# A two-layer hybrid decoder step on Trainium2: the gathered tokens' gelu values fetched as rows of 128 floats and picked out on VectorE, with filled products and the modulation in two column groups

## What is computed

```python
mod = (jax.nn.silu(c) @ p["w_ada"][l] + p["b_ada"][l])[:, None, :]
sh1, sc1, gt1, sh2, sc2, gt2 = jnp.split(mod, 6, axis=-1)
...
sv, si = lax.top_k(s, PEER_TOPK)
cand = sv[:, :, 0, :, None] + sv[:, :, 1, None, :]
best, pos = lax.top_k(cand.reshape(...), PEER_TOPK)
g = jax.nn.softmax(best, axis=-1)
act = jax.nn.gelu(jnp.einsum("thkd,td->thk", u_tab[eidx], xb).astype(jnp.float32))
return jnp.einsum("thk,thkd->td", (g * act).astype(xb.dtype), v_tab[eidx])
```

## Time and profile before

| | us |
|---|---|
| median of 3 runs | 6634.29 |
| lowest, highest | 6592.53, 6678.65 |
| the profiled execution | 6574.45 |
| its span, first to last instruction | 6572.9 |
| TensorE busy | 5772.6 (88%) |
| VectorE busy | 2340.9 (36%) |
| ScalarE busy | 808.6 (12%) |
| GpSimd busy | 1317.7 (20%) |

### The profile page before, as it was taken

How to read it: one execution, slowest core, us unless ns; L and a number is a source line. 1 busy time by engine, 2 the same in 40 slices (tenths; PEclk the granted TensorE clock), 3 DMA queues, 4 the chain that set the end, 5 groups by cost and what they waited for, 6 DMA issues and landing times.

```text
span 6572.9 us, 83990 instructions
## 1 busy us (share of the span) xinstructions
PE 5772.6 (88%) x28364; PEld 4603.0 (70%) x28364; DVE 2340.9 (36%) x5282; ACT 808.6 (12%) x1522; POOL 1317.7 (20%) x1553
## 2 busy tenths in 40 slices
PE   7999898999997788677989998989999968886688
PEld 3876775777786677566848767657777857774567
DVE  1333323219542244323403233232195313443233
ACT  1112112101231000000011121121112310000000
POOL 0000003000003355533200000030000043554332
PEclk9999997999998899788999989989999989997889
DMA  7872125524442588766878711254244426886676
GB/s 241 257 220 72 51 79 163 157 64 142 163 144 98 192 293 288 228 198 225 296 241 255 217 50 51 88 182 134 61 153 161 138 91 219 291 295 205 204 244 261
DMA packets 642553, 1169.10 MB, mean 178 GB/s; under 512 B 61073, under 2 KB 402065, under 8 KB 641249
## 3 DMA queue, kind: packets, MB, share of 16 engines
q1 hardware_dynamic: 510080, 760.84, 36.1%
q0 software_dynamic: 132192, 404.89, 18.3%
HBM read 1097.92 MB, written 201.82 MB: 198 GB/s over the span
## 4 chain that ended last, share of the span: by engine, by line
PE 78%; another core or an unknown queue 7%; issue 6%; DMA 2%; DVE 2%; SPq 2%; DVEq 1%; ACT 1%; ACTq 0%; POOLq 0%; POOL 0%
PE PS L1153 25%; PE PS L1186 14%; PE PS L579 9%; PE PS L665 7%; PE PS L1099 3%; PE PS L792 2%; PE PS L1123 2%; PE PS L1172 2%; PE PS L1118 2%; PE PS L629 1%; DMA ring<-in_wst 1%; PE PS L614 1%; PE PS L704 1%; SPq L412 1%
## 5 line engine op out<-in xcount | busy, mean ns | idle before, releaser
L1153 PE MATMUL PS<-hT,ring 128*128 128x288 f32 (+1 forms) x8192 | 1946.7, 398 | 238.9 <-ACT arena L2143 135.0
L1153 PEld LDWEIGHTS PS<-hT,ring 128*128 128x128 f32 x8192 | 1566.0, 193 | 574.0 <-ACT arena L2143 146.5
L1186 PE MATMUL PS<-arena,ring 128*128 128x256 f32 x4096 | 963.4, 392 | 293.8 <-issue 278.9
L1186 PEld LDWEIGHTS PS<-arena,ring 128*128 128x128 f32 x4096 | 804.5, 197 | 452.2 <-issue 340.5
L1920 ACT ACTIVATE arena<-PS 128x272 f32<-128x272 f32 (+7 forms) x530 | 318.2, 609 | 2795.3 <-DVEq L1908 935.4
L665 PE MATMUL PS<-hT,ring 128*128 128x272 f32 x2304 | 626.0, 418 | 0.0
L544 POOL DMA_INDIRECT arena<-gelu_rows,hT x512 | 486.1, 950 | 166.3 <-issue 149.3
L665 PEld LDWEIGHTS PS<-hT,ring 128*128 128x128 f32 x2304 | 439.8, 201 | 113.6 <-issue 31.9
L579 PE MATMUL PS<-hT,ring 128*128 128x272 f32 x2048 | 478.1, 393 | 0.0
L1767 DVE SCALAR_TENSOR_TENSOR PS<-hT,arena,PS 128x1024 f32<-128x1024 f32 x288 | 370.4, 1286 | 203.7 <-DMA hT<-v_rows,RO 116.5
L579 PEld LDWEIGHTS PS<-hT,ring 128*128 128x128 f32 x2048 | 385.4, 190 | 77.6 <-issue 0.9
(11 more groups left out here) (379 smaller groups left out, 5183.3 us busy)
## 6 DMA issues: line engine op xcount, KB each, us to landing
ring<-in_uv SPq DMA_DIRECT2D x768, 512.0 KB
ring<-in_wst SPq DMA_DIRECT2D x312, 512.0 KB
v_rows<-in_uv SPq DMA_DIRECT2D x256, 512.0 KB, 6.5
gelu_rows<-arena POOLq DMA_DIRECT2D x64, 576.0 KB, 4.2
arena<-in_ck SPq DMA_DIRECT2D x128, 256.0 KB, 4.9
arena<-in_cvv POOLq DMA_DIRECT2D x64, 256.0 KB, 4.0
hT<-in_cvv POOLq DMA_DIRECT2D x64, 256.0 KB, 5.1
gate_tiles<-arena SPq DMA_DIRECT2D x96, 136.0 KB, 3.5
```

Source lines behind the costliest of these rows:

```text
L1153: i = mm(PS[:, 2 + s % 2, 0:n], ring[:, s, c, :], src[:, c, :], start=(c == 0), stop=(c == DC - 1))
L1186: i = mm(PS[:, 2 + b, 0:TD], ring[:, s, j, :], WB[:, row, :], start=(row == 0), stop=(row == NK - 1))
```

## The change

Four things change.

1. The stored gelus get a layout of 3 rows of 128 floats per expert (two blocks of 128 tokens, and a third whose last 32 floats are the sampled tokens'). A lot of four stored tiles takes two DMAs. A pick fetches the whole row of 128 floats that holds the token's value, into `EB`, two buffers of four picks. VectorE multiplies four picks at once by the identity (or by `mask4` for the sampled tokens) and sums each row of 128, which leaves the token's own value. GpSimd issues eight picks, then rows; behind every fourth row come four more picks, and they wait (`el_us`) until the lot before last has been used. `GB` shrinks from eight buffers to four to make room for `EB`.
2. Products with 4, 16, 24 or 32 rows of contraction are given 128, the rest of them zeros of the stationary side or of the mask.
3. The modulation's pair of tiles is multiplied in two column groups: 16 products of 9x128, alternately to PSUM partitions 0 and 32.
4. The three blocks share one buffer `YT`, and the first is turned ahead of the seventh chunk.

```diff
-    GB = [AR[:, C_OH + TD * i:C_OH + TD * (i + 1)] for i in range(8)]
+    GB = [AR[:, C_OH + TD * i:C_OH + TD * (i + 1)] for i in range(4)]
+    EB = [AR[:, C_OH + 1024 + 512 * i:C_OH + 1024 + 512 * (i + 1)].rearrange("p (k t) -> p k t", k=4) for i in range(2)]
...
-                    g.dma_start(gstore[k * 2 + b], SG[b]).then_inc(ag_st[b].sem, 16)
+                    g.dma_start(gstore[k * 2 + b][:, :, 0:2 * P], SG[b][:, :, 0:2 * P]).then_inc(ag_st[b].sem, 16)
+                    g.dma_start(gstore[k * 2 + b][:, :, 2 * P:3 * P], SG[b][:, :, TG - P:TG]).then_inc(ag_st[b].sem, 16)
...
-            for n in range(2 * TSA):
-                picked_gelu(n)
+            def picked_gelus(lot):
+                if lot >= 2:
+                    g.wait_ge(el_us.sem, el_us.at(l, lot - 1))
+                    g.nop(nofuse=True)
+                for j in range(4):
+                    blk, k = gathered(4 * lot + j)
+                    g.indirect_dma_start(EB[lot % 2][:, j, :], None, gelus,
+                                         bass.IndirectOffsetOnAxis(ap=EIX[blk][:, k:k + 1].bitcast(U32), axis=0)).then_inc(el_ld[lot % 2].sem, 16)
+
+            picked_gelus(0)
+            picked_gelus(1)
             g.wait_ge(vn_ld.sem, vn_ld.at(l, 16 * NK))
             g.nop(nofuse=True)
             for n in range(NROW):
-                if n + 2 * TSA < NROW:
-                    picked_gelu(n + 2 * TSA)
...
+                if n % 4 == 3 and n // 4 + 2 < NROW // 4:
+                    picked_gelus(n // 4 + 2)
...
-            return ident[0:16, row:row + 1].to_broadcast([16, P])
+            return ident[:, row:row + 1].to_broadcast([P, P])
...
-                    for c in range(DC - 1):
-                        mm(PS[0:9, b, 0:2 * P], cT[:, c, :], ring[:, 2 * b:2 * b + 2, c, :], start=(c == 0), stop=False)
-                    for j in range(2):
-                        s = 2 * b + j
-                        mm(PS[0:9, b, j * P:(j + 1) * P], cT[:, DC - 1, :], ring[:, s, DC - 1, :], start=False, stop=(j == 1)).then_inc(ring_used[s], 1)
+                    for c in range(DC):
+                        for j in range(2):
+                            i = mm(PS[32 * j:32 * j + 9, b, 0:P], cT[:, c, :], ring[:, 2 * b + j, c, :], start=(c == 0), stop=(c == DC - 1))
+                            if c == DC - 1:
+                                i.then_inc(ring_used[2 * b + j], 1)
...
-                mm(PS[:, FS[h // 2 % 2][h % 2], 0:TP], cn("nsel")[0:16, h:h + 1].to_broadcast([16, P]), R_F[:, 0:TP],
+                mm(PS[:, FS[h // 2 % 2][h % 2], 0:TP], cn("nsel")[:, h:h + 1].to_broadcast([P, P]), ZALL[:, 3, 0:TP],
...
-            out_chunk(3, 0)
             turned(0, 0)
+            out_chunk(3, 0)
             turned(1, 1)
...
+            NV.memset(SQ[3], 0.0)
             v.drain().then_inc(hn_go.sem, 1)
...
-                    if n % TSA == 0:
-                        cols = slice(GCOL[blk] + k, GCOL[blk] + k + TSA)
-                        v.wait_ge(el_ld[n // TSA].sem, el_ld[n // TSA].at(l, 16 * TSA))
+                    if n % 4 == 0:
+                        cols, b = slice(GCOL[blk] + k, GCOL[blk] + k + 4), n // 4 % 2
+                        x0, own = (0, ident[:, :]) if blk < NT else (P - TSA, mask4)
+                        v.wait_ge(el_ld[b].sem, el_ld[b].at(l, 64 * (n // 8 + 1)))
                         v.nop(nofuse=True)
+                        picks = EB[b][:, :, x0:P]
+                        tt(picks, picks, bc(own.unsqueeze(1), [P, 4, P - x0]), ALU.mult)
+                        v.drain()
+                        NV.tensor_reduce(DOT[:, cols], picks, AX.X, ALU.add)
+                        v.drain()
                         tt(DOT[:, cols], DOT[:, cols], GW[:, cols], ALU.mult)
-                        v.drain()
+                        v.drain().then_inc(el_us.sem, 1)
...
-                copy(MT[:, bass.ds((k * 2 + b) * 256, 256)], PS[0:9, b, 0:2 * P]).then_inc(ad_s.sem, 1)
+                copy(MT[:, bass.ds((k * 2 + b) * 256, P)], PS[0:9, b, 0:P])
+                copy(MT[:, bass.ds((k * 2 + b) * 256 + P, P)], PS[32:41, b, 0:P]).then_inc(ad_s.sem, 1)
...
-                        s_.wait_ge(a_v.sem, a_v.at(l, k * 8 + (b * 4 + j + 1 - 8)))
-                        act(GB[b * 4 + j], PS[:, 2 + j % 2, 0:TD], ACT.Gelu_apprx_tanh).then_inc(gl_s.sem, 1)
+                        s_.wait_ge(a_v.sem, a_v.at(l, k * 8 + (b * 4 + j + 1 - 4)))
+                        act(GB[j], PS[:, 2 + j % 2, 0:TD], ACT.Gelu_apprx_tanh).then_inc(gl_s.sem, 1)
```

More of the change, by code:

```diff
@@ L611, in headnorm @@
                     pe.nop(nofuse=True)
-                w = ident[0:R, row:row + 1].to_broadcast([R, P]) if k == 1 else wide(10, 1024)[0:R, (n - 8) * P:(n - 7) * P]
+                w = spread(row) if k == 1 else wide(10, 1024)[:, (n - 8) * P:(n - 7) * P]
                 for hf in range(2):
-                    i = mm(PS[:, 6 - 2 * (n % 2) + hf, 0:HT], w, SQ[3][0:R, hf * HT:(hf + 1) * HT], start=True, stop=True)
+                    i = mm(PS[:, 6 - 2 * (n % 2) + hf, 0:HT], w, SQ[3][:, hf * HT:(hf + 1) * HT], start=True, stop=True)
                 i.then_inc(hn_sp.sem, 1)
@@ L753, in _ @@
                             pe.nop(nofuse=True)
-                        mm(PS[:, 6, :], kt[0:32, hs], wide(10, 1024)[0:32, 0:512], start=True, stop=True)
-                        mm(PS[:, 7, :], kt[0:32, hs], wide(10, 1024)[0:32, 512:1024], start=True, stop=True).then_inc(sd_mm.sem, 1)
+                        mm(PS[:, 6, :], kt[:, hs], wide(10, 1024)[:, 0:512], start=True, stop=True)
+                        mm(PS[:, 7, :], kt[:, hs], wide(10, 1024)[:, 512:1024], start=True, stop=True).then_inc(sd_mm.sem, 1)
                         late_upto(late_at("seq", h + 1))
@@ L771, in _ @@
             for j in range(8):
-                h, row, src = (j % 4, 12, R_B) if j < 4 else (j % 4, 8, R_E)
+                h, row, src = (j % 4, 12, 1) if j < 4 else (j % 4, 8, 4)
                 if j >= 2:
@@ L776, in _ @@
                 for hf in range(2):
-                    i = mm(PS[:, 4 + 2 * (j % 2) + hf, 0:HT], spread(row + h), src[:, hf * HT:(hf + 1) * HT], start=True, stop=True)
+                    i = mm(PS[:, 4 + 2 * (j % 2) + hf, 0:HT], spread(row + h), ZALL[:, src, hf * HT:(hf + 1) * HT], start=True, stop=True)
                 i.then_inc(bc_mm.sem, 1)
@@ L796, in _ @@
                 for h in range(H):
-                    i = mm(PS[:, 0, h * w:(h + 1) * w], spread(8 + h), R_G[:, cs], start=True, stop=True)
+                    i = mm(PS[:, 0, h * w:(h + 1) * w], spread(8 + h), ZALL[:, 2, cs], start=True, stop=True)
                 i.then_inc(g_mm.sem, 1)
@@ L929, in _ @@
                         pe.nop(nofuse=True)
-                        mm(PS[:, 6, :], W[12][0:32, hs], wide(5, 1024)[0:32, 0:512], start=True, stop=True)
-                        mm(PS[:, 7, :], W[12][0:32, hs], wide(5, 1024)[0:32, 512:1024], start=True, stop=True).then_inc(sd_mm.sem, 1)
+                        mm(PS[:, 6, :], W[12][:, hs], wide(5, 1024)[:, 0:512], start=True, stop=True)
+                        mm(PS[:, 7, :], W[12][:, hs], wide(5, 1024)[:, 512:1024], start=True, stop=True).then_inc(sd_mm.sem, 1)
             pe.wait_ge(ss_up.sem, ss_up.at(l, 8))
@@ L1203, in _ @@
                     out_chunk(d, b)
+            turned(0, 0)
             out_chunk(3, 0)
-            turned(0, 0)
             turned(1, 1)
@@ L1227, in _ @@
         cp(W[1][:, 0:1].bitcast(U32), pcol[:, 0:1])
-        ts(pcol[:, 1:2], pcol[:, 0:1], float(P), None, ALU.add)
         v.drain()
@@ L1231, in _ @@
         v.drain()
-        cp(pcol[:, 2:3], W[1][:, 0:1].bitcast(U32))
-        v.drain()
-        ts(pcol[:, 2:3], pcol[:, 2:3], float(2 * P), None, ALU.add)
+        cp(pcol[:, 1:2], W[1][:, 0:1].bitcast(U32))
         v.drain()
```

49 lines of the change are left out of this document (25 added, 24 removed).

## The result

| | before | changed |
|---|---|---|
| median, us | 6626.33 | 6426.62 |
| lowest, highest | 6592.53, 6678.65 | 6423.21, 6460.09 |
| ratio, 95% interval | | 0.970 [0.963, 0.978] |
| span of the profiled execution | 6572.9 | 6423.0 |

The change made the kernel faster by 200 us, where I had forecast 636 (5990 us). 6427 lies 7 us above my range (5890 to 6420) and almost on rival A (6430). By the two profiled executions the gain is 150 us; the two medians lie further apart, since the profiled execution of the kernel before took 6574 us, less than any of its four other runs.

A forecast was written before the change was run, and what follows sets the result against it. Picks were taken to stop TensorE in the expert stages, through late instructions. 931 us a layer (904 + 2 + 25) saves 282 and 280, modulation 28, clock 20: 6574 - 610 = 5964, forecast median 5990, range 5890 to 6420.

The forecast's parts named there:

- rival A: Expert stages: a 512-byte pick is as dear as a 4-byte one, only (a) is saved; some 6430 us, chance 0.16.
- What bounds the kernel: Dense half and output of the experts: engines wait for instructions behind picks, losing about 308 us a layer.
- 904 us: Unstopped time of a layer's dense-half and output products: 461 plus 443 us, against 1213 and 1211.
- The picks' size: Expert stages: a 512-byte pick takes 0.25 us of DMA engine time, bounded above by 0.9, so it fits.
- 228 us lost outside (a): Loss in the rest of the expert stages, per layer; 25 us a layer was kept for what comes late.
- (a): Start of the dense half, 2060 to 2170: TensorE busy 35 of 110 us during picks, 80 us lost, counted as gone.
- The order on GpSimd: Expert stages: 8 picks ahead instead of 64, then 4 per four rows; start has 10 us of picks, not 80.
- Modulation and filled products: Before the experts: column groups save 28 us (bounds 0 and 36), a higher clock 20 us (bounds 0 and 40).
- VectorE, stores, the tail: VectorE's 115 us a layer of lot work hidden; the sampled half's larger stores and shared turned-block buffer cost nothing.
- B: Expert stages: picks are cheap but lots bunch, 984 us a layer instead of 931; about 6100 us, chance 0.11.
- C: Expert stages: lots run one after another, 16.9 us each, 1301 us a layer; about 6760 us, chance 0.03.

The follow-up runs named there:

- e1: Changed kernel without its 288 gathers of gelu rows (picks) per layer: 5846 us, dense part 890 us in each layer.
- e4: Changed kernel with TensorE's 256 output products per loop body written as a loop of 32: 6467 us.
- e12: Kernel computing the reference with gelu values stored behind each expert's row, one list gather per step, 288 instead of 576 a layer: 5870 us, ratio 0.887 to the kernel before.
- e5: Changed kernel with each pick replaced by a plain DMA of 128 consecutive rows of 512 bytes: 5850 us.
- e6: Changed kernel with each pick fetching rows for 16 partitions instead of 128, by the same lists: 6583 us.
- e8: Changed kernel without picks, each gather of 4096-byte rows made as two gathers of 2048-byte rows: 6474 us.
- e11: Changed kernel with every second pick a plain DMA of 128 rows of 512 bytes, 432 list gathers a layer: 5868 us.
- e9: Kernel before with only the filled products and the modulation's column groups: 6512 us, ratio 0.985 to the kernel before.
- e2: Changed kernel with every pick fetching 4 bytes instead of 512, same lists and places: 6544 us.
- e16: The changed kernel itself, run again beside the kernel before (5940 us): 5878 us, ratio 0.990.
- e18: Changed kernel with a small plain DMA behind every fourth list gather, run where the kernel before took 6647 us: 6450 us.
- e13: Changed kernel with a small plain DMA behind every second list gather: 6057 us, with the kernel before at 5919 us.
- e15: Changed kernel with a fill and a drain on GpSimd behind every second list gather: 7865 us, with the kernel before at 5919 us.
- e17: Changed kernel with a small plain DMA behind every fourth list gather, beside the kernel before at 5940 us: 5930 us, ratio 0.997.
- e10: Changed kernel with a small plain DMA (16 rows of 128 bytes) after each list gather, 568 per layer: 6418 us.

## Why the prediction was wrong

*What bounds the kernel.* Held: 904 us was the right unstopped time (890 measured in e1), the loss is in these stages, and it comes and goes with the picks. My reading of why did not hold. I took the stop for late instructions, behind picks whose time the DMA share hides. A loop of 32 products, which repeats, stalls the same as one of 256 (e4), and e12 fills the DMA engines further without a stop. In the stopped 2742 to 2762 no instruction packet is on any queue either (only q0 has a row above), though that alone would not tell late packets from none.

*The picks' size, the step that failed.* I weighed 0.25 us against 0.9 us of DMA engine time for a 512-byte pick and took 0.25. The quantity itself was wrong: what stops the engines is how many list gathers GpSimd issues in a time, whatever each moves (e5, e6, e8, e11). A cheap pick would have helped only if TensorE had been short of DMA engine time, and it was not (e12). The change leaves the number of gathers at 576 in a layer and their spacing at 1.25 us. I had noted against rival A that "the stops don't come with rows, which have as many" descriptors. Rows alone were free because there is one list gather a step and not two, which the chunk of the earlier trace rows could not tell from a size effect. The rows of e8, in halves, stall as picks do. Of the 228 us lost outside (a) the step was to leave 25; 290 and 279 remain above the unstopped 890. With the start (a), it was to save 282 and 280 us; the two saved 33 and 43.

*The order on GpSimd.* Held in part. The start of the dense half lost its burst, 586 to 520 us a layer, 66 of the 80 expected. The rest of it, an output of 443 us, came to 660 and 647: the last chunks, free before, lost their freedom. I had not priced that the 64 picks ahead had also cleared the end.

*Modulation and filled products.* I forecast 28 + 20 = 48 us. The profiles show 28 to 37 us ahead of the first dense half and 38 to 39 between the layers' dense parts (e9 and the changed kernel, against before), 67 and 76 in all (the 30 us for the second layer in e9's expectation should read 38), and e9's median is 100 us lower [75 to 129 by its interval]. The two parts were not run apart, but the trace parts them. From its first to its last product the modulation takes 111 us in each layer before, 97 and 101 in the changed kernel, 103 and 101 in e9. So its share is 19 to 25 us: the cycle came as computed (7.1 against 7.0), and not all of the stage gained by it. From there to the sampled half of the experts the two layers together are 46 us shorter in the changed kernel and 49 in e9, and the clock in 960 to 1030 rose from 0.66 to 0.96. That is the filled products' share, sized too low at 20, and above its bound of 40.

*VectorE, stores, the tail.* Hidden, as said: VectorE is busy for 264 of 660 us in the output, and e1, with all of VectorE's lot operations, runs unstopped. The first dense product comes no later with the doubled stores (2022 us in the changed kernel) than without them (2031 in e9).

*The rivals.* A's number was met, in part by luck: it had the dense part shorter by 70 us a layer (33 and 43 measured) and the small parts worth 30 (67 to 76), and the two misses cancel. Its sentence (a 512-byte pick is as dear as a 4-byte one) nearly held: e2 says 117 us less dear. The Trainium skill (DMA: Bandwidth & Descriptors, Specifications) had spoken for the gain by its rule on pieces below 512 bytes. e2 and the changed kernel show at most those 117 us of it, and the run with 16 partitions of 512 bytes (e6, 6583) shows that the rest is not in the bytes. B and C did not occur: the lots pipeline, as e16 shows without the stall (902 and 892).

What the change is worth, then: where the stall exists, 200 us by the medians. By the profiles it is 150, 76 ahead of the dense halves and 76 in the dense parts, where the picks' start gave 130 and the output took 54 back. Where the stall does not exist it is 62 us, ratio 0.990.

## What to carry to other kernels

Count the list gathers that GpSimd issues back to back: here 13 in 20 us left the other engines alone, and 15 to 17 stopped them wherever the kernel before took some 6600 us, whatever each gather moved. Bring what is picked by the same index in one gather of a longer row, rather than in two gathers or in a "cheaper" form: where the stall exists, e12 beat both kernels at 5870 us, 11.3% below the kernel before, with 28% more bytes a row. When engines wait for "issue" beside a busy GpSimd, try the same issues as plain DMAs of the same rows first (e5); one run tells the issue and the bytes from the list.

## What the hardware showed that I had not expected

- Dense list gathers slow the start of instructions on TensorE and (but for e18) on VectorE, with nothing in the profile to wait for: TensorE's records and VectorE's operations come 1.4 us apart, and between two of VectorE's stands a register, semaphore or drain instruction, so it starts one each 0.7 us (2752 to 2756 in the changed kernel). In the output this begins 16 to 21 us after a burst does (the kernel before and the changed one). The Trainium skill (SBUF — State Buffer, Who interferes with whom) says that a DMA never contends with a compute engine. The durations of the operations here agree with it, a VectorE row takes 1.29 us in a stall and out of it; the starts do not. Where inside the chip the instructions wait was not found.
- The stall is not always there: the kernel before took 5919 and 5940 us beside e13 to e15 and beside e16 and e17, and 6591 to 6647 beside the others. What it hangs on was not settled. The record gives the same chip number for the group with e9 to e12 (kernel before 6612, 7 runs) and for e16 and e17 (5940, 9 runs), so if that is one chip, the chip alone does not decide. e12, with one gather a step, ran only where the kernel before stalled; what it gives where the stall is absent was not measured.
- A plain DMA of 128 rows of 512 bytes takes GpSimd 0.58 us, a list gather of the same 0.95, and 568 small plain ones (16 rows of 128 bytes) a layer in between cost only GpSimd's time (e10).
